# Eight instead of six Strassen tile pairs in each feed-forward block, some of them back to back

## The reference

```python
def swiglu(u, w_gate, w_up, w_down):
    return (jax.nn.silu(u @ w_gate) * (u @ w_up)) @ w_down

f = swiglu(rms_norm(h, ffn1_pre_g[l]), ffn1_w_gate[l], ffn1_w_up[l], ffn1_w_down[l])
h = h + 0.5 * rms_norm(f, ffn1_post_g[l])
```

## Time and profile before

| | |
|---|---|
| median of 3 runs | 1996.61 us (1996.44 to 1996.63) |
| profiled execution | 1996.58 us, its span 1994.8 us |
| TensorE busy | 1979.1 us (99%), 15084 matmuls |
| VectorE, ScalarE, GpSimd busy | 942.8, 832.4, 1031.4 us |
| weights read | 171.38 MB, 87 GB/s over the span |

### The profile page before, as it was taken

One profiled execution on the slowest core, in us unless ns is written; L12 is line 12 of the kernel. 1 busy time (PEld: TensorE's weight loads), 2 busy tenths in 40 slices (PEclk: granted clock), 3 DMA queues, 4 the chain that ended last, 5 costly groups with the idle time before them and its releaser, 6 DMA issues.

```text
span 1994.8 us, 35807 instructions
## 1 busy us (share of the span) xinstructions
PE 1979.1 (99%) x15084; PEld 1904.5 (95%) x15084; DVE 942.8 (47%) x1485; ACT 832.4 (42%) x1330; POOL 1031.4 (52%) x1257
## 2 busy tenths in 40 slices
PE   9999999999999999999999999999999999999998
PEld 8999999999899999999999999999998998898887
DVE  7665300478556765310076552104785467662102
ACT  6433222465555533332264332224555464442321
POOL 3655554575315655554375554545763256555551
PEclk9999999999999999999999999999999999999999
DMA  4223332122211222432122233322322112333321
GB/s 168 87 94 127 101 104 93 60 96 80 64 33 43 81 90 95 132 117 88 58 75 85 96 121 108 102 84 69 96 80 64 33 54 75 108 115 117 116 73 43
DMA packets 48480, 175.77 MB, mean 88 GB/s; under 512 B 5184, under 2 KB 9408, under 8 KB 48320
## 3 DMA queue, kind: packets, MB, share of 16 engines
q1 hardware_dynamic: 48176, 173.40, 26.6%
q10 hardware_dynamic: 144, 0.10, 0.0%
HBM read 171.38 MB, written 2.10 MB: 87 GB/s over the span
## 4 chain that ended last, share of the span: by engine, by line
PE 98%; DVE 1%; ACT 0%; DMA 0%; issue 0%; SPq 0%; DVEq 0%
PE ps L1833 97%; PE ps L2214 1%; DMA h<-in_x 0%; DVE osb L1781 0%; DVE xl L1791 0%; DVE tail_step L1322 0%; PE ps L2093 0%; ACT xh L856 0%; DVE probT L1749 0%; ACT prob L1178 0%; DVE qt L1662 0%; DVE small L1758 0%; DVE h L1327 0%; ACT tmp L1214 0%; ACT xh L1229 0%
## 5 line engine op out<-in xcount | busy, mean ns | idle before, releaser
L774 POOL TENSOR_TENSOR wlo<-raw,whi 128x256 fp32r<-128x256 f32 (+2 forms) x1148 | 946.0, 856 | 719.6 <-ACT whi L826 716.8
L1833 PE MATMUL ps<-xh,whi 128*128 128x264 f32 (+2 forms) x2616 | 632.8, 296 | 3.6 <-DVE xl L1361 1.8
L1833 PE MATMUL ps<-xl,whi 128*128 128x264 f32 (+2 forms) x2616 | 628.4, 294 | 0.0
L1833 PE MATMUL ps<-xh,wlo 128*128 128x264 f32 (+2 forms) x2616 | 627.8, 294 | 0.0
L826 ACT ACTIVATE whi<-raw 128x1024 fp32r<-128x1024 f32 (+3 forms) x337 | 363.0, 1078 | 276.9 <-PE ps L1833 240.8
L1833 PEld LDWEIGHTS ps<-xh,whi 128*128 128x128 f32 x2616 | 435.6, 188 | 17.1 <-DVE wlo L1356 2.7
L1833 PEld LDWEIGHTS ps<-xl,whi 128*128 128x128 f32 x2616 | 434.4, 188 | 10.6
L1833 PEld LDWEIGHTS ps<-xh,wlo 128*128 128x128 f32 x2616 | 434.1, 188 | 9.9
L1833 PE MATMUL ps<-hidh,whi 128*128 128x264 f32 (+2 forms) x1276 | 313.6, 296 | 0.0
L1833 PE MATMUL ps<-hidl,whi 128*128 128x264 f32 (+2 forms) x1276 | 312.4, 295 | 0.0
L1833 PE MATMUL ps<-hidh,wlo 128*128 128x264 f32 (+2 forms) x1276 | 312.4, 295 | 0.0
(11 more groups left out here) (230 smaller groups left out, 2463.2 us busy)
## 6 DMA issues: line engine op xcount, KB each, us to landing
raw<-in_ffn_up SPq DMA_DIRECT2D x88, 512.0 KB, 3.6
raw<-in_ffn_down SPq DMA_DIRECT2D x64, 704.0 KB, 4.0
raw<-in_ffn_gate SPq DMA_DIRECT2D x87, 512.0 KB, 3.6
raw<-in_w_in SPq DMA_DIRECT2D x28, 512.0 KB, 3.6
raw<-in_w_out SPq DMA_DIRECT2D x16, 512.0 KB, 3.6
raw<-in_w_q SPq DMA_DIRECT2D x8, 384.0 KB, 3.2
out_t<-h SPq DMA_DIRECT2D x16, 128.0 KB, 1.8
h<-in_x SPq DMA_DIRECT2D x2, 528.0 KB, 5.6
```

What stands on the lines that cost most here:

```text
L774: ins = nc.gpsimd.tensor_tensor(w_lo(n)[:, at], raw[:, r, at], w_hi(n)[:, at].bitcast(F32), ALU.subtract)
L1833: return nc.tensor.matmul(o, w, x, start=start, stop=stop)
```

## The change

Pairs 5, 7, 8, 10, 11, 13, 14 and 16 are Strassen pairs: 5 and 16 stand alone, (7, 8), (10, 11) and (13, 14) are couples, with one ordinary pair ("between") after each. So that the second of a couple finds its weights, the sums move: s2up of the coming pair is summed at the end of the Strassen pair before the ordinary one, and the sums of s13, s2up and s4 of a couple's second pair are made during the first. Of the second pair of a couple the s13 slot (`SECOND`) gets its low half from GpSimd; its s4 slot stays with VectorE. On ScalarE the high half of the s4 slot goes ahead of silu in a couple's first pair, `part_copy` of the second pair is issued in the first, and in an ordinary pair with a Strassen pair next the high half of the first slot ahead goes before silu.

```diff
-STRASSEN = (5, 7, 9, 11, 13, 15)
+STRASSEN = (5, 7, 8, 10, 11, 13, 14, 16)
...
+    assert not any(m + 1 in STRASSEN and m + 2 in STRASSEN for m in STRASSEN)
...
-    LO_DVE = {0, 1, 2} | {n for n in KIND if KIND[n] in ("s13", "s4")}
+    SECOND = {TILES_OF[b, m][1] for b, m in TILES_OF if m in STRASSEN and m - 1 in STRASSEN}
+    LO_DVE = {0, 1, 2} | {n for n in KIND if KIND[n] in ("s13", "s4")} - SECOND
...
                     if m in STRASSEN:
-                        part_copy(m)
+                        if m - 1 not in STRASSEN:
+                            part_copy(m)
                         for i in range(3):
                             hi(n[i] + RING)
-                        silu(m)
-                        hi(n[3] + RING)
+                        if m + 1 in STRASSEN:
+                            hi(n[3] + RING)
+                            silu(m)
+                            part_copy(m + 1)
+                        else:
+                            silu(m)
+                            hi(n[3] + RING)
                         hid_hi(m)
                         continue
+                    if m + 1 in STRASSEN:
+                        hi(n[0] + RING)
                     silu(m)
-                    if m:
+                    if m and m + 1 not in STRASSEN:
                         hi(n[0] + RING)
...
                     nxt = [i + RING for i in n]
-                    sums(nxt[0])
                     if m in STRASSEN:
-                        strassen_sums(m, 0)
-                        sums(nxt[1])
-                        low(nxt[0])
-                        sums(nxt[2])
-                        low(nxt[1])
-                        strassen_sums(m, 1)
-                        strassen_sums(m, 2)
-                        low(nxt[2])
+                        if m + 1 in STRASSEN:
+                            sums(nxt[1])
+                            strassen_sums(m, 0)
+                            sums(nxt[2])
+                            sums(nxt[3])
+                            strassen_sums(m, 1)
+                            strassen_sums(m, 2)
+                        else:
+                            strassen_sums(m, 0)
+                            strassen_sums(m, 1)
+                            strassen_sums(m, 2)
                         strassen_sums(m, 3)
                         gate(m)
                         up(m)
-                        sums(nxt[3])
+                        if m + 1 not in STRASSEN:
+                            sums(nxt[3])
                         hid(m)
+                        if m + 2 in STRASSEN and m + 1 not in STRASSEN:
+                            sums(TILES_OF[b, m + 2][2])
                         low(nxt[3])
                         hid_lo(m)
                         continue
+                    between = m - 1 in STRASSEN and m + 1 in STRASSEN
+                    if between:
+                        sums(nxt[1])
+                    else:
+                        sums(nxt[0])
                     gate(m)
...
-                    sums(nxt[1])
+                    if not between:
+                        sums(nxt[1])
```

## The result

The changed kernel takes 1984.61 us (median of 4 runs, 1984.27 to 1985.64) against 1996.62 before (1996.44 to 1997.08, 4 runs): ratio 0.9941, 95% interval 0.9928 to 0.9954, 12.0 us less where 12.4 was forecast. Its profiled execution is the longest of the four, 1985.64.

What follows compares the result with a forecast made beforehand. TensorE, busy 99% of the span, was taken to bound the kernel: 1996.58 - 11.5 (matmuls: 9.2 in three blocks, 2.3 in the last) - 0.9 (first mixer) = 1984.2 us, supply costs 0; range 1983.0 to 1991.0.

Steps and rivals of the forecast that it cites:

- The matmuls: Three blocks before the last: two more Strassen pairs each, 1.53 us saved per pair, together 9.2 us.
- The last block: Block of 512 tokens: two more Strassen pairs save 1.17 us each, together 2.3 us.
- Costs in all: 0: Supply of weights in 12 couples: no stall of TensorE; bound 0.5 us a couple, 0 to 6 us, taken as 0.
- its high half goes ahead of silu(6): Pair 6 on ScalarE: with the sum made earlier, pair 8's up weights load near t = -1 instead of 0.6.
- rival A: A small stall in each couple, 0.4 x 12 = 4.8 us, so 1989 us (1985.5 to 1991); chance 0.16.
- The mixer: First mixer: PSUM shift by two removes TensorE's 0.89 us stop for the last query's read; 0.9 us less, none in the second.
- The supply: Couples: weight halves, sums and loads for the second pair come before TensorE wants them; gate 1.1 us to spare.
- two or more over 1.1 us: Sign on VectorE: pair 8's weight sums between 4.2 and 8.2, two or more longer than 1.1 us.
- the tight point: GpSimd's third tile of a couple's second pair: ends at 15.3, wanted 15.8, 0.5 us to spare, 0.2 in the last block.
- B: GpSimd bounds the couples: third slot's low half 2.1 us late in each of 12, 25 us, so 2009; chance 0.07.
- D: VectorE's gate in a couple's first pair or the loads come late, eating the gain, 1.0 us each: 1996.6; chance 0.05.
- C: No gain in the mixer, the wait for query 7 turning up behind the next unit: 1985.1 us; chance 0.06.

Runs made afterwards that it cites:

- seven pairs: The changed kernel with seven Strassen pairs a block (5, 7, 8, 10, 12, 14, 16), so one couple: 1989.59 us, ratio 0.9965.
- the second one: Second profiled execution of the changed kernel, from running it once more with nothing edited: median 1984.46 us, ratio 0.9942; this profile 1984.40.
- order alone: The changed kernel's order on VectorE, ScalarE and GpSimd with the old six Strassen pairs (5, 7, 9, 11, 13, 15), no couples: 1997.31 us, ratio 1.0003.
- high half after silu: The changed kernel with the high half that was moved ahead of silu put back behind it, in pair 4 of each block only: 1983.27 us, ratio 0.9935.
- both repairs: The changed kernel with pair 4's high half back behind silu and the last two queries' PSUM pairs exchanged in the second mixer: 1982.39 us, ratio 0.9928.

## Why the prediction was right, and which terms were off

**The matmuls.** Of the three blocks 9.2 us were forecast. The middle part gave 6.19 for two, with its stop unchanged, and seven pairs gave half of that and the stop; the first part is 3.1 and the mixer. Right to 0.1.

By the rule of the Trainium skill (TensorE: Matmul & The Clock Gate, Back-to-back issue gap), which is for an isolated matmul and by the page's own words counts too little at small widths, the estimate was 8.1 us for the three blocks. The measured 3.1 + 6.2 doesn't agree with it, and the earlier trace rows was the better price.

**The last block is the step that was mis-sized.** The forecast had 2.3 us for it and "Costs in all: 0". It came out at 0.64 in the profiled execution and 1.55 in the second one (415.28 - 413.73); 2.36 was to be had. The supply was worked out for a couple of block 0 and its room made smaller for the shorter pairs of the last block. Left out was pair 4, ahead of all couples. The high half ahead of silu stands in the forecast only as a gain, for pair 6 ("its high half goes ahead of silu(6)"); that the same move lets GpSimd start earlier in pair 4 and meet VectorE there got no price. Behind the input sums of the last block VectorE has no idle time, and the 1.05 us of the two collisions cost TensorE 0.71, as order alone shows without any couple, or 0.81, as high half after silu shows by taking it away (413.73 - 412.92). The rest, 0.91 us, is rival A, at two of three couples and in one of two profiles: a late load at the one, the order of the turns at the other.

**The mixer.** 0.9 forecast, 1.1 found: the stop went where it was said and stayed in the second mixer. The idle time in a row is not the whole price of a stop.

**The supply.** This is where a blind forecast could have failed, and its clock times held to 0.1 us in block 0: third tile 15.3 and 15.3, gate 11.6 and 11.6, sums from 4.1 to 8.2. What did not hold was the sign "two or more over 1.1 us": one sum has 1.22, the others 1.04, 0.88 and 0.68, though the turns were taken; the length that a row shows depends on when in the other engine's turn the operation arrives. The room at the tight point was 0.5 as forecast in all nine couples of 528 tokens (0.57 from tile to load, less 0.05).

**The rivals.** B was ranked at 0.07 and did not come, but its mechanism is real: 2.0 us more on GpSimd in a couple brought a kernel slower than before. D's is real too, 1.8 us on VectorE. C did not come: the first mixer gave the whole stop. B and D stood behind one number each, 0.5 and 1.1 us of room, and the forecast was as good as these two numbers.

**The sum.** 11.07 us less without the start, 10.94 with it, where the forecast says 12.4: + 0.1 matmuls, + 0.2 mixer, - 1.7 stops of the last block add up to 11.0. The medians are 12.0 apart, nearer to the forecast: this execution was the slowest of its four.

**What stays open.** The runs without a profile can't be cut into parts, so how often the couples of the last block stop isn't known: they did in one of two profiles of the changed kernel, and in the one with both repairs. That the order of the turns decides is a reading of 16 couples, not an edit. Why a load of 512 KB takes 3.9 us once and 4.4 another time isn't shown either.

## What to carry to other kernels

Where work is moved for all blocks alike, work the cover out again for the block with the least idle time (here the last one, behind its input sums), and follow the move through to the other engines: what was moved on ScalarE cost nothing there, but GpSimd started earlier and held up VectorE. An engine that takes over work at less than half the speed costs nothing as long as its last tile is there, so what is to be worked out is the time when that tile is wanted less the time when it is done: 0.5 us of room held nine times of nine, and the last block's 0.16 only where GpSimd went first. For differences of a few tenths cut both traces at TensorE's own marks before comparing them.

## What the runs showed of the hardware

- VectorE and GpSimd, both on SBUF operands, hold each other up by whole operations, and where one started 0.01 us ahead of the other the order lasted for a pair and went with a loss of 0.35 us of TensorE. Of GpSimd's twelve quarters in pair 8 six took 1.14 to 1.22 us, the other six 0.74: the four beside the weight sums, and two of the third tile, beside the hid product and a low half. Without the sums all twelve took 0.74, since the third tile was then done before the hid product could hold it up. A meeting costs GpSimd some 0.45, the forecast's 0.44, and six of them, less some 0.3 of waits between tiles, are the step from 8.66 to 11.07.
- VectorE paid the same for an operation of either width seen: 1024 columns of a low half took 1.76 us beside GpSimd and 1.23 alone, 512 columns of a weight sum 1.22 and 0.69. So one wide operation was held up less than two narrow ones would be.
- A stop of TensorE with 0.89 us of idle time moved everything behind it by 1.03 to 1.11 us.
- The start, up to the first long piece of TensorE, varied from 11.84 to 12.66 us in twelve profiled executions of eleven kernels, on more than one chip. That is about what one of the repairs gains.
